# Attention heads in pairs and an early embedding filler in the first mixer, a gated embedding in halves, and a 128-byte start of the pool

## What is computed

```
h = h + 0.5 * rmsnorm(swiglu(rmsnorm(h, g[0]), ffn1_w_in[i], ffn1_w_out[i]), g[1])
u = rmsnorm(h, g[2])
mix = even_mixer(u, ...) if i % 2 == 0 else odd_mixer(u, ...)
h = h + rmsnorm(mix, g[3])
h = h + 0.5 * rmsnorm(swiglu(rmsnorm(h, g[4]), ffn2_w_in[i], ffn2_w_out[i]), g[5])
gate = jax.nn.sigmoid(h @ ple_w_gate[i])
h = h + rmsnorm(gate * (p[i] @ ple_w_proj[i]), g[6])
```

```
s = jnp.einsum('bnqgrd,bnkgd->bngrqk', qb, kk) * (D ** -0.5)
s = jnp.where(valid, s, -jnp.inf)
m = jnp.maximum(jnp.max(s, axis=-1, keepdims=True), sink)
pr = jnp.exp(s - m)
denom = jnp.sum(pr, axis=-1, keepdims=True) + jnp.exp(sink - m)
o = jnp.einsum('bngrqk,bnkgd->bnqgrd', pr / denom, vv)
```

## Time and profile before

| | us |
|---|---|
| median of 3 executions (range) | 1499.29 (1498.14 to 1502.18) |
| the profiled execution, its own time | 1498.02 |
| span of its trace | 1496.0 |
| PE busy, of the span | 1433.3 (96%) |
| DVE, ACT busy | 873.4 (58%), 709.1 (47%) |
| even mixer, about | 535 to 672 |
| embedding(0), FFN1 of layer 1 from about | 874, 886 |
| embedding(1) to the end | 1474 to 1496 |

### The profile page before, as it was taken

The page is one execution under the profiler, slowest core; times in us unless marked ns, Lnnn a source line. Parts: engine busy times, 40 slices in busy tenths (PEclk is TensorE's granted clock), DMA queues, the critical chain, the costliest instruction groups (busy, mean ns, idle before and its releaser), DMA issues.

```text
span 1496.0 us, 17141 instructions
## 1 busy us (share of the span) xinstructions
PE 1433.3 (96%) x6622; PEld 1182.6 (79%) x6622; DVE 873.4 (58%) x817; ACT 709.1 (47%) x701; POOL 89.9 (6%) x93
## 2 busy tenths in 40 slices
PE   5999899899999999999999989999999999999997
PEld 5788677677888877788888878888888877888885
DVE  7745775966454485665545474553775354654535
ACT  3445757435344354744444455353453444543433
POOL 0000101002000020020000010000201100200001
PEclk9999999999999999999999999999999999999999
DMA  9645333655464544335546365554555443645541
GB/s 373 242 163 220 113 113 128 250 212 210 172 224 169 197 171 148 121 118 203 203 149 230 130 246 190 203 198 168 195 179 205 156 173 133 239 152 185 190 175 43
DMA packets 40509, 272.52 MB, mean 182 GB/s; under 512 B 4865, under 2 KB 5889, under 8 KB 8834
## 3 DMA queue, kind: packets, MB, share of 16 engines
q1 hardware_dynamic: 36560, 261.49, 48.0%
q10 hardware_dynamic: 3890, 10.19, 2.0%
HBM read 270.62 MB, written 1.05 MB: 182 GB/s over the span
## 4 chain that ended last, share of the span: by engine, by line
PE 82%; DVE 10%; ACT 3%; issue 2%; DMA 2%; SPq 0%; POOL 0%; DVEq 0%; POOLq 0%; ACTq 0%
PE acc L1876 25%; PE acc L1878 25%; PE acc L1877 25%; PE turn L1929 3%; DVE wlo L1099 3%; DMA raw<-in_units 2%; ACT whi L391 1%; DVE gate_part L1500 1%; PE aux L2184 1%; DVE xn L1153 1%; DVE h L1169 1%; DVE feed_lo L1137 0%; PE turn L2034 0%; PE aux L2340 0%; PE aux L2215 0%
## 5 line engine op out<-in xcount | busy, mean ns | idle before, releaser
L1099 DVE TENSOR_TENSOR wlo<-raw,whi 128x2048 fp32r<-128x2048 f32 x233 | 533.2, 2299 | 274.8 <-ACT whi L391 274.6
L1876 PE MATMUL acc<-whi,feed_hi 128*128 128x512 f32 (+1 forms) x1504 | 600.3, 399 | 11.4 <-DVE feed_lo L1137 7.9
L1878 PE MATMUL acc<-whi,feed_lo 128*128 128x512 f32 (+1 forms) x1504 | 588.0, 391 | 0.0
L1877 PE MATMUL acc<-wlo,feed_hi 128*128 128x512 f32 (+1 forms) x1504 | 587.1, 390 | 0.0
L391 ACT ACTIVATE whi<-raw 128x2048 fp32r<-128x2048 f32 x233 | 445.6, 1917 | 283.6 <-PE acc L1878 262.6
L1876 PEld LDWEIGHTS acc<-whi,feed_hi 128*128 128x128 f32 x1504 | 285.0, 189 | 70.8 <-issue 10.1
L1878 PEld LDWEIGHTS acc<-whi,feed_lo 128*128 128x128 f32 x1504 | 284.4, 189 | 60.4
L1877 PEld LDWEIGHTS acc<-wlo,feed_hi 128*128 128x128 f32 x1504 | 285.0, 190 | 56.6 <-issue 1.2
L1876 PE MATMUL acc<-whi,hid_hi 128*128 128x512 f32 x352 | 138.0, 392 | 0.0
L1878 PE MATMUL acc<-whi,hid_lo 128*128 128x512 f32 x352 | 137.1, 389 | 0.0
L1877 PE MATMUL acc<-wlo,hid_hi 128*128 128x512 f32 x352 | 137.0, 389 | 0.0
(11 more groups left out here) (312 smaller groups left out, 872.4 us busy)
## 6 DMA issues: line engine op xcount, KB each, us to landing
raw<-in_units SPq DMA_DIRECT2D x237, 1024.0 KB, 4.9
mod_raw<-in_units SPq DMA_DIRECT2D x8, 1024.0 KB, 15.7
gpost<-in_norm_g ACTq DMA_DIRECT2D x8, 512.0 KB, 5.1
gpre<-in_norm_g ACTq DMA_DIRECT2D x6, 512.0 KB, 6.2
h<-in_x SPq DMA_DIRECT2D x1, 1024.0 KB, 7.2
w_ax<-in_w_ax SPq DMA_DIRECT2D x1, 1024.0 KB, 26.8
bgate<-in_b_gate SPq DMA_DIRECT2D x1, 1024.0 KB, 25.4
out<-h SPq DMA_DIRECT2D x2, 512.0 KB, 2.6
```

Source lines behind the costliest of these rows:

```text
L1099: dve.tensor_tensor(wlo[:, u % RING, :], raw[:, u % RING, :], whi[:, u % RING, :].bitcast(F32), ALU.subtract).then_inc(lo_ready, 1)
L1876: pe.matmul(out, xh, wh, start=first, stop=False)
L1877: pe.matmul(out, xh, wl, start=False, stop=False)
L1878: return pe.matmul(out, xl, wh, start=False, stop=last)
```

## The change

1. In the even mixer the eight heads go in four pairs (k and k + 4: query rows on partitions 0 to 63 and on 64 to 127). A pair's masks are written first, into the two banks of `aux`, then the four q·k matmuls by turns on the two halves of the rows. Maxima, sink terms and denominators are taken for two heads at once. The mix goes to the free 128 columns of the `turn` bank that holds the head's turned probabilities, and `head_out` multiplies by the reciprocal there and frees the bank; the pass over `ymix` and its wait are gone. `query` is copied without its Silu; one Silu and one Sigmoid then work on all 256 rows.
2. The slots: `ple0` comes first for both tiles (before, slots 22 and 23), now into `aux`; `ple1` comes where `ple0` was, and no filler stands among the output slots. The turn of `xn[1]` moves from slot 2 to slot 4. `pT` of layer 0 is loaded and split during FFN1.
3. Gated embedding: the squares go to the unused `hid` instead of over acc, so that DVE's gain pass (L1162) waits for the product alone. In embedding(0) the turn of `xn[0]` at t = 1 stands before the fourth unit instead of the third, and the split of the fourth unit (`hi`, `lo`) comes behind the t = 1 chain on ACT and DVE. Tile 1 is gated and squared in halves of 512 columns. In embedding(1) PE computes the first 512 columns of tile 1 for all four units, then the other 512. The output leaves in four pieces of 256 KB rather than two of 512 KB.
4. `pool_at`, where the big buffers begin in SBUF, is rounded up to 128 bytes; buffers of the mixer are laid out anew.

```diff
--- before.py
+++ after.py
-EVEN_TURNS = ("q0 k0 q1 k1 p0 f0 g0 p1 p2 p3 f1 p4 p5 g1 p6 p7 s0 s1 h0 h1").split()
-SWA_SCORES = (9, 10, 11, 12, 13, 14, 17, 18)
-SWA_TURNS = (12, 13, 14, 15, 16, 17, 20, 21)
-SWA_MIXES = (13, 14, 15, 16, 17, 18, 21, 22)
+EVEN_TURNS = ("q0 k0 q1 k1 f0 g0 p0 p4 p1 p5 f1 g1 p2 p6 p3 p7 s0 s1 h0 h1").split()
+SWA_SCORES = (11, 13, 15, 17)
+SWA_TURNS = (14, 16, 19, 21)
+SWA_MIXES = (15, 17, 20, 22)
...
-        pool_at = const_at + 4 * (C_HEADS * 3 * P + C_DV)
+        pool_at = (const_at + 4 * (C_HEADS * 3 * P + C_DV) + 127) // 128 * 128
...
+                def gate_half(half):
+                    act.activation(xn[:, 1, halves[half]], acc[1][:, halves[half]], ACT.Sigmoid).then_inc(ple_gate, 1)
+
+                def square_half(half):
+                    n["ple"] += 1
+                    act.wait_ge(ple_mul, n["ple"])
+                    act.activation(junk[:, halves[half]], xn[:, 1, halves[half]], ACT.Square,
+                                   accum_out=ss_half[:, half:half + 1]).then_inc(ss_ready if half else half_sums, 1)
...
+                square_sum(xn[:, 0, :], junk)
+                hi(2)
+                if not layer:
+                    feed(feed_hi, 0)
+                    after_h()
+                    pre_square(0, pre_junk)
+                hi()
+                if not layer:
+                    sums(1)
+                    gate_half(0)
+                    gate_half(1)
+                    square_half(0)
+                else:
+                    act.wait_ge(embed_half, 1)
+                    gate_half(0)
+                    square_half(0)
+                    sums(1)
+                    gate_half(1)
+                square_half(1)
...
+                for name in ("g0", "g1"):
+                    received(name)
+                act.activation(qsT[:, :, :], qsT[:, :, :], ACT.Silu).then_inc(q_silu, 1)
+                for name in ("f0", "f1"):
+                    received(name)
+                act.activation(fT[:, :, :], fT[:, :, :], ACT.Sigmoid).then_inc(f_sig, 1)
+                probs_turned(2)
...
+                    dve.wait_ge(sink_exp, k + 1)
+                    mark(dve.tensor_tensor(den[:, k::4, :], den[:, k::4, :], esink[:, k::4, :], ALU.add))
+                    settle()
+                    mark(dve.reciprocal(rden[:, k::4, :], den[:, k::4, :]))
+                    settle()
+                    for j in range(2):
+                        i = k + 4 * j
+                        use = turns0 + EVEN_TURNS.index(f"p{i}")
+                        dve.wait_ge(swa_mixed, 2 * k + j + 1)
+                        dve.tensor_tensor(ymix[:, :, BANK + B_HD * i:BANK + B_HD * i + B_HD],
+                                          turn[:, use % 2, 3 * P:].rearrange("p (t d) -> p t d", t=TOK),
+                                          rden[:, i, :].rearrange("p (t o) -> p t o", o=1).to_broadcast([P, TOK, B_HD]),
+                                          ALU.mult).then_inc(moved[use % 2], 1)
...
+                        if i == RING - 1:
+                            feed_normed(xn[:, 0, :] if t else h[:, 1, :])
+                        unit(u0 + i, t)
...
+                if layer:
+                    for half in range(2):
+                        for i in range(RING):
+                            s = (u0 + i) % RING
+                            for k in range(2):
+                                w = slice(D * k + BANK * half, D * k + BANK * half + BANK)
+                                ins = three(acc[1][:, BANK * half:BANK * half + BANK], feed_hi[:, 2 * i + k, lanes(1)],
+                                            feed_lo[:, 2 * i + k, lanes(1)], whi[:, s, w], wlo[:, s, w],
+                                            i == 0 and k == 0, i == RING - 1 and k == 1)
+                            if half:
+                                ins.then_inc(unit_used, 1)
+                        if not half:
+                            ins.then_inc(embed_half, 1)
...
-                    for q, keys in ((slice(0, P), slice(0, P)), (slice(P, 2 * P), slice(0, 2 * P))):
-                        cols = slice(0, P) if keys.stop == P else slice(P, 3 * P)
-                        pe.matmul(aux[:, i % 2, cols], qbT[at, i % 4, q], kbT[at, keys], start=True, stop=False)
-                        last = pe.matmul(aux[:, i % 2, cols], ident_r[:, :], bias_r[:, cols], start=False, stop=True)
+                        pe.wait_ge(ple_out, TOK)
+                    else:
+                        pe.wait_ge(swa_p, k)
+                    for j in range(2):
+                        pe.matmul(aux[:, j, 0:3 * P], ident_r[:, :], bias_r[:, :], start=True, stop=False)
+                    for cols, q, keys in ((slice(0, P), slice(0, P), slice(0, P)),
+                                          (slice(P, 3 * P), slice(P, 2 * P), slice(0, 2 * P))):
+                        for j in range(2):
+                            at = slice(B_HD * j, B_HD * j + B_HD)
+                            last = pe.matmul(aux[:, j, cols], qbT[at, k, q], kbT[at, keys], start=False,
+                                             stop=(cols.start > 0))
                     last.then_inc(swa_scored, 1)
...
-                slots = [("swa", k, k, t) for t in range(TOK) for k in range(3)]
-                slots += [("fq", 3 + k, k, t) for t in range(TOK) for k in range(4)]
-                slots += [("ig", 7 + k, k, t) for t in range(TOK) for k in range(4)]
-                slots += [("ple0", 11, 0, t) for t in range(TOK)]
-                slots += [("out_swa", 12 + k, k, t) for t in range(TOK) for k in range(2)]
-                slots += [("out_hgrn", 14 + k, k, 0) for k in range(2)] + [("ple1", 16, 0, 0)]
-                slots += [("out_hgrn", 14 + k, k, 1) for k in range(2)] + [("ple1", 16, 0, 1)]
+                slots = []
+                for t in range(TOK):
+                    slots += [("ple0", 0, 0, t)] + [("swa", 1 + k, k, t) for k in range(3)]
+                slots += [("fq", 4 + k, k, t) for t in range(TOK) for k in range(4)]
+                slots += [("ig", 8 + k, k, t) for t in range(TOK) for k in range(4)]
+                slots += [("ple1", 12, 0, t) for t in range(TOK)]
+                slots += [("out_swa", 13 + k, k, t) for t in range(TOK) for k in range(2)]
+                slots += [("out_hgrn", 15 + k, k, t) for t in range(TOK) for k in range(2)]
                 for s, (kind, k, i, t) in enumerate(slots):
-                    if i == 0 and kind not in ("out_hgrn", "ple1"):
+                    if i == 0 and kind not in ("out_hgrn", "ple0"):
                         ready(t)
-                    if s == 2:
+                    if s in (1, 5):
+                        all_moved()
+                    if s == 4:
                         feed_normed(xn[:, 1, :])
-                    if s == 3:
-                        all_moved()
-                    if s in (5, 8):
-                        rotated(0 if s == 5 else 1)
+                    if s in (6, 10):
+                        rotated(0 if s == 6 else 1)
                     if s in SWA_MIXES:
                         swa_mix(SWA_MIXES.index(s))
+                    if s == 13:
+                        forget(0)
+                        query(0)
+                    if s == 18:
+                        forget(1)
+                        query(1)
                     if s in SWA_TURNS:
                         swa_turns(SWA_TURNS.index(s))
                     if s in SWA_SCORES:
                         swa_scores(SWA_SCORES.index(s))
-                    if s == 12:
-                        forget(0)
-                        query(0)
-                    if s == 15:
-                        forget(1)
-                    if s == 18:
-                        query(1)
-                    if s == 23:
+                    if s == 25:
                         swa_fed(0)
-                    if s == 24:
+                    if s == 26:
                         hgrn_scores()
-                    if s == 25:
+                    if s == 27:
                         swa_fed(1)
                         hgrn_mix()
-                    if s in (27, 30):
-                        hgrn_fed(0 if s == 27 else 1)
+                    if s in (29, 31):
+                        hgrn_fed(0 if s == 29 else 1)
                     if s == 33:
                         normed_rows()
```

More of the change, by code:

```diff
@@ L609, in _, with embed @@
                     feed(feed_hi, 0)
+            def embed(layer):
+                act.wait_ge(ple_loaded, 16 * (layer + 1))
+                act.activation(pT_hi[layer][:, :, :], pT[layer][:, :, :], ACT.Copy).then_inc(ple_hi, 1)
             def ffn(second, layer):
@@ L670, in ffn @@
                 hidden(FF_GROUPS, 1, 2)
+                if not second and layer == 0:
+                    embed(0)
                 hi(2 * RING - 4)
@@ L689, in embedding @@
                     load_gains(gpre, io["norm_g"][1, 0:1, :], pre_loaded)
[L690 to L704, removed]
```

(34 more changed lines are left out.)

445 lines of the change are left out of this document (213 added, 232 removed).

## The result

The changed kernel takes 1490.69 us (median of 4, 1487.39 to 1491.57) against 1499.67 (4 runs): ratio 0.9941, 95% interval 0.9925 to 0.9957. It is faster, by 9.0 us where 16.3 were forecast, and 0.7 above the range. The profiled execution has a span of 1485.4 us and its own time is 1487.39, so its gain on the one of before (1498.02) is 10.6.

The account below looks back on a forecast made before the run. PE bounds the kernel, busy 1433.3 of 1496.0 us. Terms 4.6 + 3.4 + 5.3 - 4.0 - 1.9 + 2.1 + 3.8 + 2.4 = 15.7 give 1482.3 from 1498.02, up to 1483.6 for the median; forecast 1483, range 1476 to 1490.

Parts of the forecast that it names:

- Start of the pool: 0: Moved pool address: no cost, as hid_lo in the pool takes 687 ns and feed_lo outside it 685.
- rival 2: The pairs stall: waits reach 8 to 11 us, half clock at the mixer's end, 1489 to 1492 us; chance 0.13.
- Start of the mixer, 4.6: Even mixer, later turn of xn[1]: the wait of 2.93 and half clock of 1.7 go, 4.6 us gained.
- the pass over `ymix`, 3.4: Turn of the attention's result in the even mixer: PE's wait of 3.42 goes, 3.4 us gained.
- Scores, 5.3: Even mixer's paired q·k and masks: a pair takes 1.72 instead of 3.04 us, 5.3 saved in all (2.1 to 7.8).
- rival 1: Row halves run side by side: a pair's scores take 1.09 us, 7.8 saved for 5.3, 1480.5 us; chance 0.15.
- New waits, -4.0: Between the head pairs in the even mixer: PE waits for copies and banks, 4.0 us lost (1 to 8).
- (c): Slot 20: mixes wait for copies behind Silu, Sigmoid and two table loads on ACT, 1.7 us.
- End of the mixer, -1.9: Even mixer's end, one unit covering xn[0]'s chain: waits of 1.2 and 0.73, 1.9 us lost (1.5 to 3.6).
- Embedding(0), 2.1: Turn of xn[0] one unit later against waits of 1.46 and 0.73: 2.1 us gained (1.5 to 2.2).
- FFN1, 3.8: Start of layer 1's FFN1: tile 1's chain some 2.8 us earlier, waits and half clock saved, 3.8 us (2 to 4.1).
- The end, 2.4: Kernel's end, last sigmoid to end of h: 4.5 us instead of 6.92, 2.4 gained (2 to 3).

Follow-up runs that it names:

- p1: The changed kernel with the pool 128 bytes further up, so that hid and the weights both stand at 128 within 256 bytes; 1483.52 us.
- p2: The kernel before with only its pool 128 bytes further up, so that hid stands at 0 within 256 bytes; 1505.12 us, ratio 1.0043.
- s2: p1 with both heads of a pair given the first half of the rows in q·k; no kernel time given, block 1.95 us.
- p5: The changed kernel with every buffer and the pool at 0 within 256 bytes; 1482.91 us, one run.
- p3: The changed kernel with every buffer moved up by 128 bytes, weights and feed at 0 within 256 bytes, hid at 128; 1492.94 us, one run.
- s1: The changed kernel with both q·k matmuls of a pair's first head listed before both of the second; 1490.29 us.
- p4: The changed kernel without the rounding of the pool's start, hid at 224 within 256 bytes, weights at 128; 1491.27 us, one run.
- c1: p1 with the gated embedding and output as in the kernel before, the mixer as changed; 1486.97 us.
- e1: p1 with DVE's third lo in embedding(0) behind the gain pass and the fourth behind the feed of xn[1] in FFN1; 1486.07 us.
- e3: p1 with the mixer's output slots reordered and ACT's hi and DVE's lo split around the turn of HGRN's tile 1; 1482.77 us, ratio 0.9885.

## Why the prediction was wrong, step by step

- **The step that failed: "Start of the pool: 0".** It set two durations on DVE beside each other and took them to speak for the matmuls. The cost lies on PE, 5 ns in each of 1056 matmuls on `hid`, and it could not be read from the trace of before, where weights, feed and `hid` all stand alike. Measured: 7.2 us between the changed kernel and p1 (6.4 when each is set against the executions of before that were made beside it), 6.2 between before and p2. The prediction's last line did name it as a sign of being wrong ("if the same instructions run slower or faster in buffers that were laid out anew"), but without a price or a chance. The measured time lies in the band of rival 2, whose stalls didn't come. With the address repaired the kernel takes 1483.52, where 1483 was forecast. That agreement is partly luck, since the steps below missed in both directions.
- *Start of the mixer, 4.6, and the pass over `ymix`, 3.4.* Right: no idle time at either, and no half clock there in any trace of the changed mixer.
- *Scores, 5.3.* Short, and the overlap was wrong: 3.04 less 1.30 to 1.39 is 1.68 a pair, 6.7 in all. The expected block of 1.72 was made of one head's stream after the other; where they do go one after the other (s2), the block takes 1.95 to 2.03, and side by side they hide each other. That is rival 1, which had 0.15 and in its turn priced the block too low, at 1.09.
- *New waits, -4.0.* Over-sized: 1.05 + 0.26. Only (c) came, and smaller.
- *End of the mixer, -1.9.* Right for this execution: 1.36 + 0.73, and 0.31 ahead of the next stage. The half clock that I left out is not in it; it is in the trace of p5, 3.41 us at 656.94, behind the same two waits, and likewise in p3, s1 and s2, but not in p1, p4, c1 and e1. So four of nine traces with these slots have it, and the prediction counted it as a sign of being wrong.
- *Embedding(0), 2.1.* Right: 2.65 by the starts of equal matmuls, from its first (859.2 in the trace of before; the 874 in the table of times lies in its second tile) to the first of FFN1.
- *FFN1, 3.8.* Mis-sized: only 0.74 more by the starts of equal matmuls. The step said that `hi` and `lo` go behind the chain. It overlooked that another `lo` still ends at 878.65 ahead of the products, and that the moved one then stands ahead of the feed (1.54). Its 1.7 for the half clock rested on one execution: the stretch is gone in the trace of the changed kernel, but it is back, 3.41 or 6.83 us long, in all seven other traces with this embedding (p1, p3, p4, p5, s1, s2, e3), and missing in p2 and c1, which have the old one.
- *The end, 2.4.* Right, with some luck: 2.76, of which 2.2 lie in the chain up to the end of `h` and 0.6 in the last transfer, which the forecast left as it was.

Summed by the profiled executions, the mixer gives 4.6 + 3.4 + 6.7 - 1.3 - 2.4 = 11.0, embedding with FFN1 and end 3.4 + 2.8, the address takes 5.6; that leaves 11.6, of which 10.6 arrived. The odd mixer lost about half a microsecond more, around its output, which also reads a buffer of the pool. The median of the changed kernel is 3.3 above its profiled execution, where the forecast allowed 1.27: that one had a mean clock of 0.996, the other three 0.990 to 0.992, and a half-clock stretch costs 1.7. Where these fell in the other three is not recorded. A hint: all eleven later traces have at least one half-clock stretch between 160 and 270 us, in the first block, which the change doesn't touch, and the profiled executions of before and after have none there.

## What to carry to other kernels

Where an address changes, look at the pace of every instruction that reads there, on every engine, not at one duration that is at hand; compare windows of equal work by their count. Put the operands of the matmuls that bound a kernel at equal places (here within 256 bytes), and check it again after any small tensor is added ahead of them. A piece that is moved out of one wait has to be followed to the next thing that needs it: both a `lo` behind a chain and a `hi` ahead of it became the new wait. Count a half clock as won or lost only where several traces agree; one execution shows too little.

## What was not expected of the hardware

- A matmul whose two SBUF operands stand differently within 256 bytes (by 96 or 128) is 5 to 7 ns slower at 512 columns (392 to 397 and 399 ns), with nothing waiting.
- Matmuls on the two halves of the rows start 6 to 14 ns apart and share their time (0.85 instead of 1.50 us for four), even where the list has both of one half first.
- The same two waits of PE, 1.36 and 0.73 us at the end of the mixer, are followed by a half clock (3.41 us at 0.50) in four of nine traces and not in the other five.
